# Scores of a cached key page: one multiply over all heads and one sum, in place of one multiply-and-sum per head

## What is computed

```
s_past = jnp.einsum('bthd,bshd->bhts', q, k_past, preferred_element_type=jnp.float32) * scale
s_past = s_past + cq[..., None] + tail.transpose(0, 2, 1)[:, :, None, :]
p = jax.nn.softmax(jnp.concatenate([s_past, s_new], axis=-1), axis=-1)
```

```
s = jnp.einsum('bthd,bmhd->bhtm', q, mk, preferred_element_type=jnp.float32) * (X_HEAD_DIM ** -0.5)
```

## Time and profile before

| what | us |
|---|---|
| median of three runs | 1842.69 |
| lowest and highest of them | 1839.71, 1845.56 |
| span of the profiled execution | 1838.9 |
| PE, DVE, ACT, POOL busy in it | 1581.3, 1037.4, 631.3, 242.0 |

### The profile page before, as it was taken

The page is one execution under the profiler, slowest core; times in us unless marked ns, Lnnn a source line. Parts: engine busy times, 40 slices in busy tenths (PEclk is TensorE's granted clock), DMA queues, the critical chain, the costliest instruction groups (busy, mean ns, idle before and its releaser), DMA issues.

```text
span 1838.9 us, 33832 instructions
## 1 busy us (share of the span) xinstructions
PE 1581.3 (86%) x12263; PEld 1455.3 (79%) x12263; DVE 1037.4 (56%) x3203; ACT 631.3 (34%) x730; POOL 242.0 (13%) x379
## 2 busy tenths in 40 slices
PE   5999989783966667879777699999999999999996
PEld 4999868772743444569756699999999999999996
DVE  5557858567685887464663544444344444444444
ACT  5333313222241331333343344444233333333332
POOL 1000122121212222212103300000000000000332
PEclk9999989886977757789878799999999999999998
DMA  7456899886968688564342244554455554554553
GB/s 271 175 190 246 328 348 402 335 347 211 324 201 314 205 299 287 205 258 182 115 138 76 93 179 180 182 181 175 141 178 189 192 180 179 181 181 141 180 181 117
DMA packets 88612, 390.28 MB, mean 212 GB/s; under 512 B 9144, under 2 KB 22208, under 8 KB 66640
## 3 DMA queue, kind: packets, MB, share of 16 engines
q1 hardware_dynamic: 39824, 233.98, 35.4%
q0 software_dynamic: 39376, 143.15, 21.4%
q10 hardware_dynamic: 9328, 12.13, 1.9%
HBM read 379.13 MB, written 10.10 MB: 212 GB/s over the span
## 4 chain that ended last, share of the span: by engine, by line
PE 62%; DVE 14%; DMA 5%; issue 4%; ACT 2%; POOLq 1%; POOL 0%; DVEq 0%; ACTq 0%
PE bank L1388 18%; PE bank L1389 18%; PE bank L1390 18%; DVE page L933 4%; DMA page<-vc_dram 3%; DVE wlo L834 2%; DMA page<-kc_dram 2%; PE bank L1492 2%; ACT whi L492 1%; PE bank L1583 1%; DVE hl L873 1%; DMA g_s<-s_dram 1%; DMA nb<-mem_fm_dram 1%; DVE nb L888 1%; DVE g_dd L1099 0%
## 5 line engine op out<-in xcount | busy, mean ns | idle before, releaser
L1388 PE MATMUL bank<-hh,whi 128*128 128x264 f32 (+1 forms) x2688 | 779.3, 290 | 40.4 <-DVE hl L873 21.3
L1389 PE MATMUL bank<-hl,whi 128*128 128x264 f32 (+1 forms) x2688 | 770.9, 287 | 0.0
L1390 PE MATMUL bank<-hh,wlo 128*128 128x264 f32 (+1 forms) x2688 | 770.0, 286 | 0.0
L834 DVE TENSOR_TENSOR wlo<-raw,whi 128x2048 fp32r<-128x2048 f32 (+1 forms) x232 | 491.8, 2120 | 405.4 <-ACT whi L492 405.1
L492 ACT ACTIVATE whi<-raw 128x2048 fp32r<-128x2048 f32 (+1 forms) x232 | 410.4, 1769 | 837.8 <-PE bank L1390 833.7
L1388 PEld LDWEIGHTS bank<-hh,whi 128*128 128x128 f32 x2688 | 516.4, 192 | 55.0 <-issue 35.3
L1389 PEld LDWEIGHTS bank<-hl,whi 128*128 128x128 f32 x2688 | 517.0, 192 | 0.7 <-issue 0.7
L1390 PEld LDWEIGHTS bank<-hh,wlo 128*128 128x128 f32 x2688 | 514.1, 191 | 0.0
L933 DVE CUSTOM_DVE_ANT_0 page<-page,qb 128x128 f32<-128x128 f32 x1024 | 225.6, 285 | 70.8 <-DMA page<-kc_dram 52.4
L1388 PE MATMUL bank<-f_hi,whi 128*128 128x264 f32 x704 | 202.5, 288 | 7.5 <-DVE f_lo L1364 7.5
L1390 PE MATMUL bank<-f_hi,wlo 128*128 128x264 f32 x704 | 201.7, 287 | 0.0
(11 more groups left out here) (247 smaller groups left out, 1057.0 us busy)
## 6 DMA issues: line engine op xcount, KB each, us to landing
raw<-p_gu_dram SPq DMA_DIRECT2D x88, 1024.0 KB, 4.8
page<-kc_dram POOLq DMA_DIRECT2D x128, 512.0 KB, 6.2
page<-vc_dram POOLq DMA_DIRECT2D x128, 512.0 KB, 6.3
raw<-p_dn_dram SPq DMA_DIRECT2D x64, 704.0 KB, 4.1
raw<-p_fox_dram SPq DMA_DIRECT2D x24, 1024.0 KB, 4.8
raw<-p_gla_dram SPq DMA_DIRECT2D x24, 1024.0 KB, 7.7
raw<-p_out_dram SPq DMA_DIRECT2D x16, 1024.0 KB, 4.9
raw<-p_mem_dram SPq DMA_DIRECT2D x8, 1024.0 KB, 8.3
```

The lines of the kernel that those rows point to most:

```text
L834: tt(wlo[:, k % 4, 0:blocks * P], raw[:, k % 4, 0:blocks * P], whi[:, k % 2, 0:blocks * P], ALU.subtract).then_inc(S("w_split"), 1)
L1388: mm(out, blk(whi, k % 2, b), rh, start=start, stop=False)
L1389: mm(out, blk(whi, k % 2, b), rl, start=False, stop=False)
L1390: return mm(out, blk(wlo, k, b), rh, start=False, stop=stop)
```

## The change

`k_page` becomes two instructions per page: `k_mul` multiplies the whole page (8 x 128 elements per partition) in place with the query, and `k_sum` sums each head's 128 products with one reduction into the eight scores. `k_page(t, j)` now issues the multiply of page `j` and then the sum of page `j - 1`; the sum of page 15 is issued by `s_max`. The semaphore `k_used`, which frees the slot, is raised by the sum. A new semaphore `k_mul` stands between a multiply and its sum. `x_scores` becomes one multiply, with the query repeated for both halves, a wait for it, and one sum.

```diff
--- before.py
+++ after.py
@@ -923,19 +923,33 @@
 
             tail4 = tail[:, :].rearrange("p (h b j) -> p j b h", h=H, b=ND)
 
+            def k_slot(t, j):
+
+                q = j if isinstance(t, int) and t == 0 else MIX.index(("k", j))
+                return q, q % SLOTS
+
+            def k_mul(t, j):
+
+                q, slot = k_slot(t, j)
+                dve.wait_ge(S(f"page_in{slot}"), arrived(t, q))
+                tt(page[:, slot, :], page[:, slot, :], qb[:, :], ALU.mult).then_inc(S("k_mul"), 1)
+
+            def k_sum(t, j):
+
+                _, slot = k_slot(t, j)
+                own("k_mul", 16 * t + j + 1)
+                dve.tensor_reduce(s_raw[:, j, :], page[:, slot, :].rearrange("p (h d) -> p h d", h=H), AX.X, ALU.add
+                                  ).then_inc(S("k_used"), 1)
+
             def k_page(t, j):
 
-                q = j if isinstance(t, int) and t == 0 else MIX.index(("k", j))
-                slot = q % SLOTS
-                dve.wait_ge(S(f"page_in{slot}"), arrived(t, q))
-                for h in range(H):
-                    pk = page[:, slot, P * h:P * h + P]
-                    ins = dve.tensor_tensor_reduce(out=pk, in0=pk, in1=qb[:, P * h:P * h + P], scale=1.0, scalar=0.0,
-                                                   op0=ALU.mult, op1=ALU.add, accum_out=s_raw[:, j, h:h + 1])
-                ins.then_inc(S("k_used"), 1)
+                k_mul(t, j)
+                if j:
+                    k_sum(t, j - 1)
 
             def s_max(t):
 
+                k_sum(t, PAGES - 1)
                 own("k_used", 16 * t + 16)
                 ch.link(tt(s_bias.rearrange("p (j b) h -> p j b h", b=1), s_raw.rearrange("p (j b) h -> p j b h", b=1),
                            tail4[:, :, ds(t, 1), :], ALU.add))
@@ -1267,12 +1281,11 @@
             def x_scores(b):
                 dve.wait_ge(S("xq_b"), b + 1)
                 dve.wait_ge(S(f"page_in{b}"), 16 * 33)
-                for m in range(2):
-                    for h in range(XH):
-                        pk = page[:, b, 512 * m + P * h:512 * m + P * h + P]
-                        ins = dve.tensor_tensor_reduce(out=pk, in0=pk, in1=x_qb[:, b % 2, P * h:P * h + P], scale=1.0, scalar=0.0,
-                                                       op0=ALU.mult, op1=ALU.add, accum_out=x_s[:, b, m, h:h + 1])
-                ins.then_inc(S("xk_used"), 1)
+                tt(page[:, b, :].rearrange("p (m n) -> p m n", m=2), page[:, b, :].rearrange("p (m n) -> p m n", m=2),
+                   row(x_qb[:, b % 2, :]).broadcast_to([P, 2, 512]), ALU.mult).then_inc(S("xk_mul"), 1)
+                own("xk_mul", b + 1)
+                dve.tensor_reduce(x_s[:, b, :, :].rearrange("p m h -> p (m h)"),
+                                  page[:, b, :].rearrange("p (m d) -> p m d", m=2 * XH), AX.X, ALU.add).then_inc(S("xk_used"), 1)
 
             f_start(0, False)
             f_start(1, False)
```

## The result

The changed kernel takes 1906.58 us (three runs, 1903.34 to 1913.68) against 1842.69: a ratio of 1.0362 with a 95% interval of 1.0335 to 1.0389 (1.0347 by the two medians alone), 64 us slower. The forecast was 1916, +73. The profiled execution has a span of 1904.7 us, 65.8 above the one of before.

A forecast was written before the change was run, and what follows sets the result against it. The bound was read stage by stage: mostly TensorE's panel matmuls, with VectorE full in the turns' first halves. Terms 1.7 + 27.6 + 21.7 + 18 + 4 = 73 on a 1838.9 span gave 1911.9, so 1916 us; range 1870 to 1956.

The forecast's parts named there:

- The page: VectorE's time per key page in the scoring: 2.28 us instead of 1.70, between 1.75 and 2.38; +0.58 us a page.
- Sample 0: VectorE's idle time in the panels covers 16 x 0.58; the end, page and query multiply, is not covered: +1.7 us.
- Samples 1 to 3: VectorE's longer first steps, and slots given back late making TensorE wait for value pages: 9.2 us a turn, +27.6.
- Sample 4: Norm part +3.5 us; then late slots make TensorE wait 5.1 for values every other panel; +21.7 in all.
- Samples 5 to 7: 9.3 us of VectorE time a turn, some pages already waiting for DMA; 6 a turn taken, +18 us.
- two thirds: Share taken of the 9.3 us of VectorE time a turn in samples 5 to 7: 6 us a turn.
- Cross attention: 8 x 0.58 us plus a 0.1 wait between multiply and sum, partly hidden: +4 us, ends 2.5 and 6.
- Fewer instructions to fetch: I count nothing: Whole kernel, end of the sum: having fewer instructions to fetch was given no time.
- swallowed holds: Rival: slots come late but the DMA backlog clears, only VectorE's own time shows; +39.5, 1882 us; chance 0.26.
- Compounding: Rival: late slots cost every stage its upper end, through POOL's order and the slow clock; +112, 1955 us; chance 0.09.
- faster: Rival: small instructions' fixed cost is real, large ones overlap as well; -0.48 us a page, -21, 1822 us; chance 0.05.
- nothing: Rival: VectorE is not the bound, all hides behind TensorE; 1843 us; chance 0.03.

The follow-up runs named there:

- Experiment 9: The changed kernel with each page's multiply and sum cut per head into eight and eight instructions of 128 elements; 1990.73 us, ratio 1.0807.
- experiment 4: The kernel before with VectorE's two loops (samples 2 and 3, 5 and 6) written out, old instructions; 1824.47 us, ratio 0.9904.
- experiment 8: The changed kernel with each page's sum directly behind its own multiply and VectorE's two loops written out; 1867.88 us, ratio 1.0142.
- experiment 6: The changed kernel with each sum directly behind its own multiply in sample 4 alone; 1890.00 us, ratio 1.0278.
- 1: The changed kernel with each page's sum directly behind its own multiply in all samples; 1873.97 us, ratio 1.0170.
- 3: The kernel before, old instructions, but each page's slot given back only after the next page's scores; 1885.74 us, ratio 1.0222.
- 2: The kernel before with only the cross attention's new `x_scores`; 1843.70 us, ratio 1.0012.
- 10: The changed kernel with only the sum of a page cut into eight of 128 elements; 1937.49 us, ratio 1.0512.
- 5: The changed kernel with VectorE's two loops (samples 2 and 3, 5 and 6) written out; 1901.12 us, ratio 1.0330.

## Why the prediction came out as it did

**The page: right.** 2.28 us was forecast from a multiply's starts, with the sum of 1024 taken as long as the multiply; it is 2.27. Counting starts, not durations, decided the sign: by durations a page would have become half a microsecond cheaper. Experiment 9 shows the reason behind it. Cut into separate multiplies and sums, a page takes 3.17 us; the old fused pair of instructions takes 0.21 a head, 1.70 a page, little more than one multiply alone (0.20). So breaking up the fused pair costs 3.17 - 1.70 = 1.47 us a page, a whole pass over the data, and merging the eight heads of both passes gives back 3.17 - 2.27 = 0.90. The change did both, and 0.57 is left. The Trainium skill ("VectorE: DVE Perf Modes", The TRN2 errata) puts the fixed price of an instruction at some 150 cycles, by its clock of 0.96 GHz an estimate of 0.16 us; from start to start experiment 9 shows 0.07, less than half of it.

**Sample 0: cover right, end under-sized.** The hundred microseconds of panels did hide the longer pages. At the end the query's multiply came 2.4 later (204.03 instead of 201.61; 1.7 was forecast), and then TensorE spread the query more slowly. TensorE's timeline of before, and of after:

```profile
202.88 1.98 PE L1438 MATMUL bank<-qd,kst 128*128 128x512 f32 x4 [2.58 <-DVE qd L921]
```

```profile
205.30 3.78 PE L1451 MATMUL bank<-qd,kst 128*128 128x512 f32 x4 [4.39 <-DVE qd L921]
```

The window of the changed kernel there has a granted clock of 0.53, mostly the lower of the two levels, 1.2 GHz; in the kernel before, in the second line, it was 1.00, though TensorE had waited there too, 2.58 us:

```profile
203.00:210.30 7.30, 5.00 (x12) 2.73 (x13) 2.15 (x5) 1.18 (x3) 0.53 (x1) 0.53 1.06 390
...
200.70:206.10 5.40, 3.22 (x16) 2.16 (x17) 2.06 (x4) 1.20 (x3) 0.53 (x1) 1.00 1.08 345
```

The 1.8 between 1.98 and 3.78 is not the change's for certain: from score maximum to page this place took 6.9 us in experiment 4, where the code there is the old one, and 5.4 in experiment 8, where it is the new.

**Samples 1 to 3: right in kind and nearly in size, but for the jump; step by step, not.** 27.6 was forecast, 25.2 is there without the jump (30.9 in experiment 6, whose code is the same there). The first step is 7.5 us long (213.72 to 221.23), as written. The forecast had 4.5 of holds in a turn beside VectorE's time; late slots against slots in time (the changed kernel against 1) is 13.3 in three turns, 4.4 each, by one execution of either. The steps came out otherwise than written. TensorE in sample 2 of the changed kernel, at values 5, 10, and 11 to 15:

```profile
329.83 1.08 PE L1505 MATMUL bank<-page,prob 128*32 128x256 f32 x8 [3.15 <-DMA page<-vc_dram]
...
346.14 1.08 PE L1505 MATMUL bank<-page,prob 128*32 128x256 f32 x8 [4.57 <-DMA page<-vc_dram]
...
354.37 2.37 PE L1505 MATMUL bank<-page,prob 128*32 128x256 f32 x40
```

The new wait for value 5 is there, 3.15 (3.96 in sample 3) where 4.8 was forecast. But the old wait of 4.45, at value 10, was to go for the most part, and it stayed: 4.57, and 5.90 in sample 3. Value 10 is fetched at 337.73 and TensorE has it 8.4 us later, not 5.5. And the wait forecast behind it, for values 13 and 15, is missing in sample 2. The last values still end 7.5 us later in the turn than before, where 7 was forecast: errors on either side that cancel, and so luck.

**Sample 4: right, by its own steps.** 21.9 against 21.7: 3.3 in the norm's part (3.5) and 18.6 after it (18.2). The trace of the changed kernel shows the loop that was worked out, first VectorE, then POOL, then TensorE:

```profile
504.78 0.42 DVE L1069 COPY mkv<-bank 128x256 f32<-128x256 f32 x1 [4.59 <-PE bank L1403]
506.72 2.29 DVE L834 TENSOR_TENSOR wlo<-raw,whi 128x2048 fp32r<-128x2048 f32 x1 [1.52 <-ACT whi L492]
508.93 1.22 DVE L935 TENSOR_TENSOR page<-page,qb 128x1024 f32<-128x1024 f32 x1
510.07 1.21 DVE L941 TENSOR_REDUCE s_raw<-page 128x8 f32<-128x1024 f32 x1
511.63 0.42 DVE L1069 COPY mkv<-bank 128x256 f32<-128x256 f32 x1 [0.35 <-PE bank L1403]
...
527.40 0.42 DVE L1069 COPY mkv<-bank 128x256 f32<-128x256 f32 x1 [9.27 <-PE bank L1403]
```

```profile
511.93 0.53 POOL L375 DMA_DIRECT2D page<-vc_dram  x1 [8.01 <-DVE s_raw L941]
```

```profile
496.82 1.08 PE L1505 MATMUL bank<-page,prob 128*32 128x256 f32 x8 [2.60 <-DMA page<-vc_dram]
...
518.40 1.08 PE L1505 MATMUL bank<-page,prob 128*32 128x256 f32 x8 [6.24 <-DMA page<-vc_dram]
...
539.48 1.08 PE L1505 MATMUL bank<-page,prob 128*32 128x256 f32 x8 [4.70 <-DMA page<-vc_dram]
```

The key page's sum stands behind evacuation, split and the next multiply and ends at 511.28; POOL, which had waited 8.01 us for it, fetches the value page at 511.93; TensorE gets it at 518.40 after 6.24 us. Three such waits, every other panel, of 2.60, 6.24 and 4.70 (5.1 was forecast). The upper end of 28 that was written for this stage does not follow from its terms, 3.5, 21.3 and 1.2, which give 26; the forecast does not use it. That the late slots are what costs here was shown both ways: undone in sample 4 alone they give back 16.6 us (6), and alone, on the old instructions, they cost 17.4 (3).

**Samples 5 to 7: right as far as the traces tell.** 20.8 without the jump against 18; experiment 6, whose code is the same there, has 15.1 without it, so whether two thirds was too little is open. By its kind it is VectorE's own time rather than slots: in experiment 1 the three turns take 280 us, no less than the 278 of the changed kernel, and in 3, with late slots and old instructions, 268.

**Cross attention: about right.** +4 was forecast; 1 to 5 is what the runs bear out. The feed-forward is unchanged.

**The step that failed** is the last one of the sum, "Fewer instructions to fetch: I count nothing". It was worth -11.5 in the trace and some -12 in time, and explains why the kernel came out at +64 instead of the +77 of the other terms. Those had been put at 73; that they came out 4 higher, against the missing 11.5, brought the total nearer to the forecast than this step deserved. What was missed stood in the trace of before: 16.1 us of VectorE's idle before L933 ended in "issue", 12.6 of it in two waits at the same place of two loops, and the change takes away most of the bodies' instructions. The Trainium skill ("Runtime: NRT & Kernel Launch", Instruction fetch mechanics) says that a taken branch to a place outside the two blocks of 256 instructions at hand has to fetch first. The traces agree as far as they go: long bodies stall, short ones don't, and the page of the profile has 44 packets on its queue for instructions with the old kernel, 23 with the changed one, 45 with 9 and 38 with 4, whose loops are written out. Of the kernel before and of the changed one (packets, MB, share):

```profile
q14 instruction: 44, 0.36, 0.1%
...
q14 instruction: 23, 0.19, 0.0%
```

Each of the eight stalls in the kernel before and in experiments 2, 3 and 9 has one of these packets inside it, some 2 us before its end (in the kernel before at 353.1, in a stall from 349.80 to 355.16, and at 593.1, in the one above); 10 has none at either jump. The changed kernel, 1 and 6 have one close to the first jump without a stall, and the trace does not say which engine's instructions a packet carries. So that the stall is that fetch is likely, not shown; what is shown is that it comes with the length of the body and goes with the loop.

Of the rivals, swallowed holds would have been 1882: 1 shows what VectorE's time without late slots costs, 1874, with the wait and the short jumps in it; late slots then add 33, so they were not swallowed. Compounding (1955), faster (1822) and nothing (1843) are all some 48 us or more from the 1906.58. Still open: whether writing out the loops gives the changed kernel more than its 0.5 and 0.6 us at the jumps. 5 and 8 were 5.5 and 6.1 lower than their counterparts, with an uncertainty of about the same size.

## What to carry to other kernels

Count instructions by start to start, in the trace, before merging them: a fused multiply-and-sum reads its data once, and splitting it into two large passes loses more than the fixed price of eight small instructions. When work is reordered, follow what gives a buffer back: moving one release behind the next page cost half of what this change lost, and half of that again in panels where VectorE had time to spare. And look at the idle time that ends in "issue" at the head of a loop: writing out two loops of two turns is worth more here (1%) than anything that was tried on the instructions in them.

## What the runs showed of the hardware

VectorE stood idle 4.7 to 7.0 us at a jump back to the head of a loop with 286 and 340 instructions of work in the body (the kernel before, experiments 2, 3 and 9), and 0.5 to 0.6 with 62 to 228; no kernel lay between 228 and 286. In float32 an instruction of 128 elements a partition costs VectorE 0.20 us from start to start, for a multiply and for a sum alike, and 0.21 for both fused with the read of the accumulator; one of 1024 costs 1.13. A sum of 1024 that waits for the multiply directly before it starts 0.1 us later than one that need not (experiment 1).
